# A hybrid decoder step: cached keys turned in 32x32 blocks by VectorE, scores as 32x32 products, and the recurrence's first 17 steps one to a piece

## The reference, cut to what matters

```python
def make_sample_fox(k_past, v_past, logf_past):
    def attn(q, k, v, logf):
        r_past = lax.cumsum(lp, axis=1, reverse=True) - lp
        return fox_attend(q, c_new, ((k_past, v_past, -r_past, past_mask), (k, v, c_new, new_mask)))
# fox_attend: s = q_t.k_s / sqrt(64) + c_q[t] - c_k[s]; softmax over all keys; times values
k_past = cache_k[l][page_table].reshape(DB, n_pages * PAGE_SIZE, FOX_HEADS, HEAD_DIM)
def wkv_step(S, inp):
    sa = jnp.einsum('bhij,bhj->bhi', S, a_t)
    S = S * w_t[:, :, None, :] + sa[..., None] * b_t[:, :, None, :] + v_t[..., None] * k_t[:, :, None, :]
    y = jnp.einsum('bhij,bhj->bhi', S, r_t)
```

## Time and profile before

| | |
|---|---|
| median of three runs | 1509.98 us |
| the profiled execution | 1510.73 us, of which the span of instructions is 1509.0 us |
| TensorE, matmuls | busy 1402.4 us, 93% of the span, 11595 instructions |
| TensorE, weight loads | busy 953.3 us, beside the matmuls |
| VectorE | 438.2 us, 29% |
| ScalarE | 357.0 us, 24% |
| GpSimd | 110.0 us, 7% |
| granted TensorE clock, mean | 0.969 of full speed |
| transfers | 219.32 MB, mean 145 GB/s |

### The profile page before, as it was taken

The page is one execution under the profiler, slowest core; times in us unless marked ns, Lnnn a source line. Parts: engine busy times, 40 slices in busy tenths (PEclk is TensorE's granted clock), DMA queues, the critical chain, the costliest instruction groups (busy, mean ns, idle before and its releaser), DMA issues.

```text
span 1509.0 us, 27895 instructions
## 1 busy us (share of the span) xinstructions
PE 1402.4 (93%) x11595; PEld 953.3 (63%) x11595; DVE 438.2 (29%) x917; ACT 357.0 (24%) x713; POOL 110.0 (7%) x223
## 2 busy tenths in 40 slices
PE   5999999988799999999989779999999999999997
PEld 4755666655577777777755454477777777744442
DVE  5022355455844444444445241310000000000002
ACT  3010233245444343443433331100000000000011
POOL 6283000000000000001202010000000000000000
PEclk9999899998799999999989889999999999999998
DMA  5187011023898787878957897003111221150001
GB/s 206 57 189 205 7 57 35 1 75 110 284 312 277 229 292 247 294 255 266 272 191 261 315 314 245 1 13 100 56 56 56 89 79 56 56 195 0 0 0 63
DMA packets 123174, 219.32 MB, mean 145 GB/s; under 512 B 11451, under 2 KB 35078, under 8 KB 123046
## 3 DMA queue, kind: packets, MB, share of 16 engines
q1 hardware_dynamic: 115154, 193.64, 38.3%
q0 software_dynamic: 7824, 23.85, 5.9%
q10 hardware_dynamic: 68, 0.02, 0.0%
HBM read 203.06 MB, written 14.41 MB: 144 GB/s over the span
## 4 chain that ended last, share of the span: by engine, by line
PE 84%; DVE 5%; DMA 4%; ACT 3%; issue 2%; SPq 1%; POOL 0%; DVEq 0%; POOLq 0%; ACTq 0%
PE PS L1369 23%; PE PS L736 13%; PE PS L1388 10%; PE PS L1178 6%; PE PS L1192 4%; PE PS L1308 4%; PE PS L1237 4%; PE PS L709 2%; DMA arena<-in_cache_k 2%; DMA out_wkv_prompt<-arena 1%; PE PS L1394 1%; PE PS L992 1%; PE PS L1002 1%; PE PS L996 1%; ACT arena L1622 1%
## 5 line engine op out<-in xcount | busy, mean ns | idle before, releaser
L1369 PE MATMUL PS<-arena 128*128 128x288 f32 x1408 | 342.1, 405 | 1.2 <-DVE arena L2251 1.2
L1369 PEld LDWEIGHTS PS<-arena 128*128 128x128 f32 x1408 | 265.7, 189 | 77.4 <-DVE arena L2251 1.4
L736 PE MATMUL PS<-arena 128*128 128x301 f32 (+1 forms) x736 | 197.7, 426 | 0.0
L1622 ACT ACTIVATE arena<-PS 128x512 f32<-128x512 f32 x256 | 141.4, 596 | 192.8 <-PE PS L1178 192.4
L1178 PE MATMUL PS<-arena 128*128 128x128 f32 x1024 | 153.8, 296 | 27.1 <-DMA arena<-in_cache_k 15.1
L736 PEld LDWEIGHTS PS<-arena 128*128 128x128 f32 (+1 forms) x736 | 136.6, 189 | 54.7 <-issue 13.6
L1178 PEld LDWEIGHTS PS<-arena 128*128 128x128 f32 x1024 | 122.1, 151 | 55.8 <-issue 24.2
L1388 PE MATMUL PS<-arena 128*128 128x512 f32 x352 | 151.5, 592 | 1.5 <-DVE arena L2277 1.5
L1388 PEld LDWEIGHTS PS<-arena 128*128 128x128 f32 x352 | 66.5, 189 | 86.2 <-issue 84.3
L2277 DVE TENSOR_TENSOR arena<-PS,arena 128x576 f32<-128x576 f32 x22 | 16.7, 758 | 327.0 <-ACT arena L1686 327.0
L1686 ACT ACTIVATE arena<-PS 128x576 f32<-128x576 f32 x22 | 14.3, 651 | 329.8 <-PE PS L1369 329.8
(11 more groups left out here) (360 smaller groups left out, 1409.9 us busy)
## 6 DMA issues: line engine op xcount, KB each, us to landing
arena<-in_cache_k SPq DMA_DIRECT2D x256, 256.0 KB, 4.3
arena<-in_cache_v SPq DMA_DIRECT2D x256, 256.0 KB, 4.8
arena<-in_w_gate SPq DMA_DIRECT2D x11, 1024.0 KB
arena<-in_w_up SPq DMA_DIRECT2D x11, 1024.0 KB
arena<-in_w_in SPq DMA_DIRECT2D x5, 2048.0 KB, 11.9
forgets_after<-arena POOLq DMA_DIRECT2D x64, 128.0 KB, 8.5
arena<-forgets_after SPq DMA_DIRECT2D x32, 256.0 KB, 5.1
arena<-in_w_down SPq DMA_DIRECT2D x4, 2048.0 KB
```

What stands on the lines that cost most here:

```text
L736: ins = mm(PS[0:width, bank, 0:HALF], wring[:, c % 2, k, c0:c0 + width], xnT[:, k, half * HALF:(half + 1) * HALF], start=(k == 0), stop=(k ...
L1369: ins = mm(PS[:, 4 * (f % 2) + 2 * w + half, 0:HO], fring[r % FR][:, c:c + P], hT[:, k, half * HO:(half + 1) * HO], start=(k == 0), stop=( ...
L1622: av(KTs[:, (2 * i + q) % LOT], PS[:, T_USE[("k", L, i, q)] % 2, :].rearrange("p (g n) -> p g n", g=NG), ACT.Copy)\
```

## The change

Keys are no longer transposed on TensorE. VectorE transposes each loaded block of 128x1024 (one page of each of the two sequences) in place, in blocks of 32x32 (turn_keys, four of them a lot). The scores are then products with 32 rows (32 channels of a head, in one of four row groups of the array) by 32 columns (queries), with 64 keys moving: 32 of each of two pages. Half a lot's scores are two parts of 64 such products, and a part uses two of the four row groups, each of which writes its own bank of PSUM. The queries get a layout for that: VectorE spreads them over the partitions in 16 small copies in the prompt's attention (QX), and ScalarE fills the stationary operand from it, once for a pair of sequences (QS, in the tile of sel, which VectorE clears first). The scores' bias is added in two halves, one for each bank. ScalarE copies the transposed probabilities, where VectorE did, and exponentiates a lot's scores in that lot's piece 6, where it was piece 1 of the next. Keys are loaded by halves of a lot into three buffers of four pages, where there was one buffer with four places of two pages. The dummy product is gone. The low-rank weights go to another tile, and their load waits for log_ready. The 17 preparing steps of the recurrence come one after each of the first 17 pieces; the other 123 are spread up to piece 236 as before.

```diff
-        QB = new(DB, NG, 32)
+        QX = new(DB, H, 2, DS)
...
-            return min(N_RWKV, 1 + piece * (N_RWKV - 1) // (8 * LOTS - 20))
+            if piece < N_PRE:
+                return 1 + piece
+            return min(N_RWKV, N_PRE + (piece - N_PRE) * (N_RWKV - N_PRE) // (8 * LOTS - 20 - N_PRE))
...
             sp.wait_ge(S["xs_ready"], NTILE)
+            sp.wait_ge(S["log_ready"], 1)
...
+            def load_bias(L):
+                if L >= 2:
+                    sp.wait_ge(S["sc_taken"], 2 * (L - 1))
+                pr, j = L // NLOT, L % NLOT
+                sp.dma_start(Rr[:, L % 2, :], biases[pr * P:(pr + 1) * P, LOTC * j:LOTC * (j + 1)]).then_inc(S[f"r_in{L % 2}"], 16)
+            def key_half(L, hh, numbers):
+                n = 2 * L + hh
+                sp.wait_ge(S["k_free"], 3 + max(n - 2, 0))
+                for i in range(2):
+                    for q in range(2):
+                        sp.dma_start(KH[n % 3][:, i, q, :], k_pages[bass.ds(numbers[q][2 * hh + i], 1)].rearrange("o p n -> p (o n)"))\
+                            .then_inc(k_in[n % 3], 16)
+            def value_page(L, i, numbers):
+                sp.wait_ge(S["v_free"], LOT * L + i + 1)
                 for q in range(2):
-                    sp.dma_start(ring[:, i, q, :], pages[bass.ds(numbers[q][i], 1)].rearrange("o p n -> p (o n)"))\
-                        .then_inc(landed[i], 16)
-            biases = forgets_after.rearrange("b r n -> (b r) n")
-            def load_bias(pr, j):
-                if j >= 2 or not isinstance(pr, int):
-                    sp.wait_ge(S["sc_taken"], pr * NLOT + (j - 1))
-                elif j == 1:
-                    sp.wait_ge(S["lr_taken"], 8)
-                sp.dma_start(Rr[:, j % 2, :], biases[bass.ds(pr * P, P), LOTC * j:LOTC * (j + 1)]).then_inc(S[f"r_in{j % 2}"], 16)
-            def key_page(pr, j, numbers, i):
-                sp.wait_ge(S["k_free"], pr * (2 * NPG) + (2 * LOT * j + 2 * i + 2))
-                load_pair(k_pages, Kr, "k_free", k_in, numbers, i)
-            def value_page(pr, j, numbers, i):
-                sp.wait_ge(S["v_free"], pr * NPG + (LOT * j + i + 1))
-                load_pair(v_pages, Vr, "v_free", v_in, numbers, i)
-            def lot_numbers(pr, j):
-                return [page_numbers(pr * 2 + q, LOT * j) for q in range(2)]
-            def load_lot(pr, j, vpr, vj, value_numbers):
-                first = isinstance(pr, int) and j == 1
-                if not first:
-                    load_bias(pr, j)
-                numbers = lot_numbers(pr, j)
-                for i in range(3):
-                    key_page(pr, j, numbers, i)
-                if vj is not None:
-                    for i in range(2):
-                        value_page(vpr, vj, value_numbers, i)
-                key_page(pr, j, numbers, 3)
-                if vj is not None:
-                    for i in range(2, LOT):
-                        value_page(vpr, vj, value_numbers, i)
-                if first:
-                    load_bias(pr, j)
-                return numbers
+                    sp.dma_start(Vr[:, i, q, :], v_pages[bass.ds(numbers[q][i], 1)].rearrange("o p n -> p (o n)")).then_inc(v_in[i], 16)
+            def lot_numbers(L):
...
+            of_lot = lot_numbers(0)
+            sp.wait_ge(S["k_free"], 3)
+            for hh in range(2):
+                key_half(0, hh, of_lot)
+            load_bias(0)
+            after = lot_numbers(1)
+            key_half(1, 0, after)
+            for L in range(LOTS):
+                if L and L + 1 < LOTS:
+                    key_half(L + 1, 1, after)
+                for i in range(LOT):
+                    value_page(L, i, of_lot)
+                if L + 1 < LOTS:
+                    load_bias(L + 1)
+                    if not L:
+                        key_half(L + 1, 1, after)
+                    of_lot = after
+                if L + 2 < LOTS:
+                    after = lot_numbers(L + 2)
+                    key_half(L + 2, 0, after)
...
+            def page_scores(L, hh, part):
+                n = 2 * L + hh
+                if part == 0:
+                    if hh == 0:
+                        if L % NLOT == 0:
+                            pe.wait_ge(S["nmn_ready"], L // NLOT + 1)
+                        if L:
+                            pe.wait_ge(S["sc_taken"], 2 * L)
+                    pe.wait_ge(S["kt_ready"], 2 * n + 2)
+                else:
+                    pe.wait_ge(S["sc_part"], n + 1)
+                a0 = 2 * (part ^ hh)
+                for hm in range(4):
+                    for d in range(2):
+                        for a in (a0, a0 + 1):
+                            for q in range(2):
+                                for gp in range(2):
+                                    h = 4 * gp + hm
+                                    o = PS[ROWS[2 * q + gp], SCORE[a % 2], 2 * P * hh:2 * P * hh + 2 * P].rearrange("p (i n) -> p i n", i=2)
+                                    ins = mm(o[:, :, 32 * a:32 * a + 32], QS[ROWS[a], q, h, d],
+                                             KH[n % 3][ROWS[a], :, q, 64 * h + 32 * d:64 * h + 32 * d + 32],
+                                             start=(hm + d == 0), stop=(hm + d == 4), skip_group_check=True)
+                ins.then_inc(S["k_free"] if part else S["sc_part"], 1)
...
-                if half:
-                    mm(PS[:, OUT, 511:512], ident, ones[:, 0:1], start=False, stop=True, skip_group_check=True).then_inc(S["ov_ready"], 1)
...
-                    turn_keys(L, 0)
-                    yield
-                    turn_keys(L, 1)
-                    page_scores(L, 0)
-                    yield
+                    page_scores(L, 0, 0)
                     if L:
                         turn_probs(L - 1)
                     yield
-                    turn_keys(L, 2)
-                    page_scores(L, 1)
+                    page_scores(L, 0, 1)
                     yield
                     if L:
                         lot_values(L - 1, 0)
                     if j == 0:
                         turn_new(pr)
                     yield
-                    turn_keys(L, 3)
-                    page_scores(L, 2)
-                    yield
                     if L:
                         lot_values(L - 1, 1)
                     yield
-                    page_scores(L, 3)
+                    page_scores(L, 1, 0)
+                    yield
+                    if j == 0 and L:
+                        turn_output(pr - 1)
+                    page_scores(L, 1, 1)
+                    yield
                     if j == 0:
-                        if L:
-                            turn_output(pr - 1)
                         new_values(pr)
+                    yield
                     if j == NLOT - 1 and pr + 1 < NPAIR:
                         new_scores(pr + 1)
                     yield
...
-            def take_keys(L, i):
-                for q in range(2):
-                    act.wait_ge(S["k_free"], 2 * LOT * (L + 1) + 2 * i + q + 1)
-                    if L or i >= 2:
-                        act.wait_ge(S["sc_page"], LOT * L + i - 1)
-                    av(KTs[:, (2 * i + q) % LOT], PS[:, T_USE[("k", L, i, q)] % 2, :].rearrange("p (g n) -> p g n", g=NG), ACT.Copy)\
-                        .then_inc(S["kt_taken"], 1)
+            def take_probs(L):
+                act.wait_ge(S["pr_turned"], L + 1)
+                av(PTs, PS[:, TURN, :].rearrange("p (a n) -> p a n", a=LOT), ACT.Copy).then_inc(S["pr_taken"], 1)
+            def fill_queries(pr):
+                if pr:
+                    act.wait_ge(S["k_free"], 3 + 2 * pr * NLOT)
+                else:
+                    act.wait_ge(S["qx_ready"], 1)
+                to = QS.rearrange("p q (b m) d n -> p (q b) m d n", m=4)
+                of = QX[:, 2 * pr:2 * pr + 2].rearrange("p q (b m) d t -> p (q b) m d t", m=4)
+                for m in range(4):
+                    ins = av(to[:, :, m, :, 8 * m:8 * m + 8], of[:, :, m], ACT.Copy)
+                ins.then_inc(S["qs_ready"], 1)
...
                     if L and j == 0:
                         exp_new(pr)
                     yield
+                    if L:
+                        take_probs(L - 1)
+                    yield
+                    yield
+                    yield
+                    yield
+                    if j == NLOT - 1 and pr + 1 < NPAIR:
+                        fill_queries(pr + 1)
+                    yield
+                    exp_lot(L)
+                    yield
+                    yield
+            fill_queries(0)
...
+            def spread_queries(n):
+                a, c = n // 4, n % 4
+                ins = v.tensor_copy(QX[ROWS[a], :, c // 2::2, c % 2, :], samps(qT[ROWS[c]]).rearrange("p g b t -> p b g t"))
+                if n == 15:
+                    ins.then_inc(S["qx_ready"], 1)
...
+            def turn_keys(n, i):
```

(32 more changed lines are left out.)

141 lines of the change are left out of this document (49 added, 92 removed).

## The result

The changed kernel takes **1820.9 us** (median of 4 runs, 1814.1 to 1828.5), the kernel before 1510.6 in the same series: ratio 1.206 [1.200, 1.211]. The forecast was 1490, range 1430 to 1560.

A forecast was written before the change was run, and what follows sets the result against it. TensorE's work was taken to bound the kernel at 16.8 us a lot. With 15.6 after the change, 27 lots save 1.2 each (32), less 11 at the start: 21 us off 1510.7, forecast 1490 us, range 1430 to 1560.

The forecast's parts named there:

- a part is 1.1 us: TensorE's new scores: 128 instructions over eight array tiles, each reused after 60 ns, plus a switch: 1.1 us a part.
- TensorE's lot of 13.3: TensorE's work a lot after the change: 7.0 us for the lot plus 6.3 of recurrence, instead of 16.0.
- Rival 4: Slower: tiles don't overlap beyond four, or instructions don't come fast enough; a part 2.1 us, 1598 us in all; chance 0.11.
- Rival 3: Idle gaps in every lot lower TensorE's granted clock to 0.93, costing 0.9 us a lot: 1514 us; chance 0.10.
- the forecast's 2.3 us of idle time in a lot: TensorE's idle time within the 15.6 us lot, beside 13.3 of work: about 1.5 ahead of piece 0's scores, 0.8 other.
- Rival 6: Slower: a floor on instruction starts, taken at 31 ns, makes a part 4.1 us: 1814 us; chance 0.03.
- VectorE's transpose: VectorE's turning of each 128x1024 key block, four a lot, was taken to cost 1.2 us each.
- rival 5: Slower: VectorE's key transpose takes 2.4 us, so VectorE has 16.7 us a lot: 1554 us; chance 0.10.
- The forecast's second way to 1.2: VectorE's transpose estimated from the skill's 311 ns for 128x128, scaled to 1024 columns less a fixed part: 1.2 us.
- TensorE's wait that ends on the transposes: TensorE idles about 1.5 us a lot ahead of piece 0's scores, until VectorE's queued transpose releases it.
- DMA as the bound: The wait is hidden and DMA bounds the lots at 14.0 us each: 1446 us; chance 0.20.
- The start: First lots: VectorE starts 5 to 7 us later, waiting for half a lot's keys; the start loses about 11 us.

The follow-up runs named there:

- run 2: Changed kernel, but from the second lot on each score product moves 2 columns instead of 64: 1813 us.
- run 4: Kernel before, with 512 one-column 32x32 filler products a lot added ahead of the real scores: 1963 us.
- run 5: Changed kernel with each part's 128 products cut into four chunks, spread between TensorE's other work of pieces 0 to 5: 1823 us.
- run 15: Kernel before, plus once after the last lot 2048 small 32x32 products as a loop of 32 rounds: 1553 us; the products took 37 us.
- run 10: Kernel before, plus once after the last lot a train of 2048 32x32 products (67 us), then 2048 128x128 ones (437 us), all one-column: 2014 us.
- run 11: Kernel before, with TensorE made to wait once a lot for seven VectorE reductions, no TensorE instruction added: 1742 us.
- run 12: Changed kernel with a quarter of its score products, transposes and waits kept: 1542 us, ratio 1.017 to the kernel before.
- run 14: Changed kernel with a quarter of its score products, and each VectorE key transpose turning 32 columns instead of 1024: 1508 us.
- run 1: Changed kernel with half of its score products, leaving out half of each head's channels: 1625 us.
- run 3: Changed kernel with half the score instructions but the same columns: first half's parts one product each, second half's products moving their columns twice: 1713 us.
- run 6: Changed kernel with half of its score products, in chunks spread over pieces 0 to 5: 1623 us.
- run 7: Changed kernel with the recurrence's steps handed out evenly over the pieces, as before the change: 1816 us.
- run 13: Changed kernel with value pages of every lot but the first loaded for only 8 of 128 partitions: 1767 us.
- run 8: Kernel before, with the recurrence's 17 first steps one to each piece, as in the changed kernel: ratio 1.013, 1529 us.
- The halves: Changed kernel with half of its score products, in bursts (1625 us) or spread over pieces 0 to 5 (1623 us).
- run 9: Kernel before, with 128 one-column 32x32 filler products a lot added ahead of the real scores: 1564 us, ratio 1.035.

## Why the prediction was wrong

- **The step that failed: "a part is 1.1 us", and with it TensorE's lot of 13.3.** Measured: 1.41 at full clock when its instructions are there, so tiles do overlap beyond four, at 11 ns and not 7.5. That size alone is worth little: by the forecast's own rule, 1.4 us a part gives a lot of 16.8 us, about 1522 us in all. What was wrong is the sum behind it, TensorE's lot of 13.3 us, which adds up durations at full clock and puts the arrival of instructions at nothing. By the table a lot's products come 26.9 a microsecond with this load of the DMA, and some 720 to 740 of them need the lot's 27.4 us. Runs 2, 4, 5 and 15 show that neither columns nor order make this pace, but the fetch.
- **Rival 4 had the mechanism and the wrong price.** I took q8's time in transfer, 1.05 us a packet, for the distance between packets (the train's in its full stretch take 1.1 us each too, by the share of 1.0%), and found it "just what a part would eat". The distance is 3.5 us at best and 6.8 beside full queues (run 10). The check that was missing is a count for the whole lot: 128 products need a block, the kernel before used one in 128 / 15.4 = 8.3 us and showed no strain; my own forecast, with about 720 products in 15.6 us, asked for one in 2.8.
- **Rival 3, the clock, was priced at 7%.** Measured 0.65 with TensorE 78% busy, and 0.82 without any new instruction (run 11). TensorE's busy time a lot went from 16.1 to 21.4 us although the change takes work away. The lot's idle time rose by 4.2 us (1.8 to 6.0), and the rest of the 9.5 us is busy time at the lower clock. Idle time explains a part of that clock: at 15 to 28% idle, the table has 0.82 without small products (run 11), 0.75 and 0.79 with a quarter of them (12, 14), 0.71 to 0.74 with half (1, 3, 6), 0.61 to 0.67 with all of the change's (changed, 2, 5, 7, 13), and 0.74 with as many fillers beside the old work (4). So many small products seem to lower it beyond their stalls; no run here separates the two. Whether the forecast's 2.3 us of idle time in a lot would have kept the full clock no run shows; run 12, nearest to it, has 3.6 us and 0.75.
- **Rival 6** came to 1814, nearly the measured time, by a floor on starts. That is a coincidence: within a part products start 11 ns apart here. The rule behind it, from the Trainium skill, "TensorE: Matmul & The Clock Gate", section "Wait — 56ns, not 53.3ns?", gives 25 ns; the rows at L1181 disagree, as that of L992 did.
- **VectorE's transpose: right.** 1231 ns against 1.2; rival 5 is out. With run 14's 204 ns for 32 columns that is 1.04 ns a column and 0.17 us fixed. The forecast's second way to 1.2 took off a fixed part that it did not name; these two sizes give it. TensorE's wait that ends on the transposes exists, as forecast, but in the changed kernel it is 7.6 us of the window, 0.5 a lot where 1.5 was forecast, under the stalls; the transposing itself is worth 1.1 us a lot once most stalls are gone (runs 12 and 14).
- **DMA as the bound: right to reject.** The share fell from 0.81 to 0.51; in 345 to 1225 SP's queue waited 499.5 us for the scores (L1181) to free the keys' buffers.
- **The start: wrong in size and reason.** The forecast had VectorE 5 to 7 us late for want of a whole half of keys; with the old steps (run 7) the first row maximum comes at 357.8, before it was 358.4, so that costs nothing. The 17 steps make it 372.3 in run 8 and 372.2 in the changed kernel. Lot 3's addition, forecast at 431, starts at 438.4 in run 8, 19 us late by the steps alone, at 441.5 in run 7, 22 us late by the stalls alone, and at 461.4 in the changed kernel, which has both. The seven steps gained for it bought nothing.

What stays open: how much of a lot is arrival and how much the clock. The halves take 21.0 us a lot where arrival at the changed kernel's pace asks for 17.3. That pace is from a DMA share of 0.51, though, and theirs is 0.66. Between 4.8 us a block at 0.51 and the train's 6.8 at 0.96, an estimate for 0.66 is 5.4 us, 19.7 for 464 products; run 9 gets a block each 6.0 us at 0.75. What is left is idle time and clock, and no run holds the clock fixed.

## What to carry to other kernels

Before cutting large products into many small ones, count TensorE's instructions (a load and a product each) in the stretch, divide by 256, and compare the time with one block in about 5 us beside a half-loaded DMA, 3.5 at best and 7 with full queues. Beyond that point a written-out product costs its share of the block, 27 to 53 ns by the train; in a loop it does not. And price a new idle stretch at TensorE at more than its length: 1.6 times in run 11.

## What was not expected of the hardware

One-column products, 128x128 ones in the train and 32x32 ones in the loop, left TensorE 100% busy and yet at the lower level of its clock. In the train it had fallen before, in a half full of stalls, and stayed there through 437 us of work without a gap (213 ns a product). Filler products of 13 ns each turned into 28 ns when four times as many. TensorE's instructions and the data share the DMA engines, so weights on their way slowed a train of products that read none of them.
